# Calls of a two-block transformer kernel in another order on four engines, with triangular products and convolutions at each head's begin

## What is computed

```
# block 1
h = rms_norm(x, pre_w);  proj = h @ w_in               # 1024 x 6152
sb:  z = q k^T / 8;  log_a = log_sigmoid(z) + suffix sum of -softplus(z)   (causal)
     o_sb = (exp(log_a) @ v) * silu(gate)
gdn: q, k, v = silu(causal_depthwise_conv(qkv, conv_w));  q, k l2-normalized
     m = strict_lower(beta * k k^T * decay);  u, w = solve(I + m, [v beta, k beta exp(g)])
     for each chunk: v_new = u - w S;  o = q exp(g) S + intra v_new;  S = S exp(g_last) + k^T v_new
     o_g = rms_norm(o) * silu(gate)
y = (sigmoid(ma) * (o_sb @ w_sb) + sigmoid(mb) * (o_g @ w_gdn)) @ w_out;  x = x + rms_norm(y)

# block 2
h = rmsnorm(x);  proj = h @ w_in_2
diff: 4 heads, each of two softmaxes of 64:  o = rmsnorm((softmax(z1 + bias) - lam softmax(z2 + bias)) @ v)
fox:  8 heads of 64: softmax(q k^T / 8 + cum_q - cum_k) @ v     (cum: running sum of log sigmoid)
x = x + rmsnorm(concat(diff, fox) @ w_out_2)
x = x + rmsnorm(square(relu(rmsnorm(x) @ w_up)) @ w_down)
```

## Time and profile before

| | us |
|---|---|
| median of 3 runs | 1246.92 |
| lowest and highest | 1245.46, 1247.05 |
| the profiled execution | 1248.23 |
| its span | 1246.9 |
| TensorE busy in the span | 1188.6 (95%) |
| ScalarE, VectorE, GpSimd busy | 557.8, 518.8, 471.6 |

### The profile page before, as it was taken

One profiled execution on the slowest core, in us unless ns is written; L12 is line 12 of the kernel. 1 busy time (PEld: TensorE's weight loads), 2 busy tenths in 40 slices (PEclk: granted clock), 3 DMA queues, 4 the chain that ended last, 5 costly groups with the idle time before them and its releaser, 6 DMA issues.

```text
span 1246.9 us, 15061 instructions
## 1 busy us (share of the span) xinstructions
PE 1188.6 (95%) x5783; PEld 931.0 (75%) x5783; DVE 518.8 (42%) x1092; ACT 557.8 (45%) x1012; POOL 471.6 (38%) x291
## 2 busy tenths in 40 slices
PE   6999999999989999989999999989899999999997
PEld 6777767767657788878677777657888888888886
DVE  4057376575564314153233333332621111644444
ACT  5356466375477653243344444343432222433332
POOL 3344344234343344552222221222444444644441
PEclk9999999999999999989999999978899999999999
DMA  8221120211121233622111111111233333423211
GB/s 240 77 68 52 35 80 23 68 52 34 51 68 35 68 102 102 219 68 56 51 52 51 52 51 51 52 51 51 68 102 93 93 101 101 127 93 102 95 58 68
DMA packets 139801, 95.35 MB, mean 76 GB/s; under 512 B 8801, under 2 KB 124874, under 8 KB 139730
## 3 DMA queue, kind: packets, MB, share of 16 engines
q1 hardware_dynamic: 136112, 89.18, 24.5%
q10 hardware_dynamic: 3618, 5.22, 1.3%
HBM read 91.49 MB, written 2.88 MB: 76 GB/s over the span
## 4 chain that ended last, share of the span: by engine, by line
PE 84%; DVE 8%; ACT 4%; POOL 1%; issue 1%; DMA 0%; ACTq 0%; DVEq 0%
PE bank L411 24%; PE bank L1166 12%; PE bank L1148 12%; PE bank L440 5%; PE bank L808 4%; PE bank L817 3%; PE bank L833 2%; DVE g L1865 2%; PE bank L946 2%; PE bank L631 2%; PE bank L1179 1%; PE bank L958 1%; PE bank L622 1%; DVE g L1862 1%; PE bank L447 1%
## 5 line engine op out<-in xcount | busy, mean ns | idle before, releaser
L2388 POOL TENSOR_TENSOR ring<-raw_ring,ring 128x1024 fp32r<-128x1024 f32 x159 | 386.3, 2433 | 607.0 <-ACT ring L1192 607.0
L411 PE MATMUL bank<-hT,ring 128*128 128x512 f32 x1536 | 406.4, 410 | 4.1 <-POOL ring L2388 3.4
L411 PEld LDWEIGHTS bank<-hT,ring 128*128 128x128 f32 x1536 | 282.7, 192 | 75.0 <-issue 16.4
L1192 ACT CAST ring<-raw_ring 128x1024 fp32r<-128x1024 f32 x160 | 166.7, 1044 | 116.2 <-PE bank L1166 93.8
L1166 PE MATMUL bank<-ring,ring_u 128*128 128x512 f32 x672 | 154.0, 391 | 0.0
L1148 PE MATMUL bank<-hT,ring 128*128 128x512 f32 x672 | 152.5, 389 | 0.0
L1166 PEld LDWEIGHTS bank<-ring,ring_u 128*128 128x128 f32 x672 | 126.2, 188 | 27.6
L1148 PEld LDWEIGHTS bank<-hT,ring 128*128 128x128 f32 x672 | 126.1, 188 | 26.1
L2365 DVE TENSOR_TENSOR ring_u<-u,ring_u 128x1024 fp32r<-128x1024 f32 x32 | 82.4, 2582 | 76.0 <-ACT ring_u L1744 76.0
L2370 DVE TENSOR_TENSOR u<-u 128x512 f32<-128x512 f32 x32 | 22.9, 715 | 139.2 <-ACT u L1751 139.2
L440 PE MATMUL bank<-hT,ring 128*128 128x256 f32 x576 | 70.4, 284 | 2.3 <-DVE hT L1790 2.3
(11 more groups left out here) (297 smaller groups left out, 1615.2 us busy)
## 6 DMA issues: line engine op xcount, KB each, us to landing
raw_ring<-in_w_in SPq DMA_DIRECT2D x144, 256.0 KB, 3.3
raw_ring<-in_w_up SPq DMA_DIRECT2D x64, 256.0 KB, 3.3
raw_ring<-in_w_down SPq DMA_DIRECT2D x64, 256.0 KB, 2.8
raw_ring<-in_w_out SPq DMA_DIRECT2D x32, 256.0 KB, 2.8
x<-in_x SPq DMA_DIRECT2D x4, 512.0 KB, 5.7
raw_ring<-in_w_branch_sb SPq DMA_DIRECT2D x8, 256.0 KB, 2.9
raw_ring<-in_w_branch_gdn SPq DMA_DIRECT2D x8, 256.0 KB, 3.3
x<-in_x ACTq DMA_DIRECT2D x4, 512.0 KB, 6.0
```

The costliest lines, as they stand in the source:

```text
L411: p = pe.matmul(bank, m.slab_k8(n % 4)[:, a, k, :], m.hT[:, b, k, :], start=term == 0, stop=term == 23)
L1192: act.copy(m.ring[:, q, 0, :], m.raw_ring[:, q, :]).then_inc(s.slab_hi[q], 1)
L2388: pool.tensor_tensor(m.ring[:, q, 1, :], m.raw_ring[:, q, :], m.ring[:, q, 0, :].bitcast(F32), ALU.subtract).then_inc(s.slab_lo[q], 1)
```

## The change

No arithmetic is changed and no instruction is added or removed: TensorE runs the same 2400 matmuls of cover and the same small calls. The calls of TensorE, ScalarE, VectorE and GpSimd inside the heads of both blocks stand in another order, and the numbers in `tiles.to(n)` are others. In block 1 `stick_v_rows` moves to the begin of the head, `stick_av` of one head stands between the `stick_z` of the two, `delta_q_sum` comes 56 matmuls into the cover and not 48, and `stick_log` in the last head follows 33 cover matmuls after `stick_z`. On ScalarE `tile_a(g + 6)` moves ahead of `delta_out_high`, and the gate's silu to other places. In block 2 the differential head's half n = 1 starts first, and `fox_z(0)` comes after 37 cover matmuls. In the last head the 72 cover matmuls are spread to its end. At the start ScalarE casts slab 1, slab 0 and squares a third block of x before it copies the columns of the norm weights (`colp`), and VectorE makes slab 1's low part before it scales the second block of x. At the end the cast `split_u(31)` stands before the last weight's. The cover is cut into 218 stretches, 188 before. The line numbers of TensorE's calls after `Tall` in the changed kernel differ from before by up to 8, those of ScalarE by 21.

The diff, cut to what is spoken of:

```diff
@@ -642,61 +641,67 @@
 
     for i in range(3):
         tiles = Tall(SLABS_A + 8 * (i + 1), 8, tile_a_free(8 * (i + 1)))
-        tiles.to(14)
+        tiles.to(10)
+        stick_v_rows(i)
+        tiles.to(27)
         delta_decay(i)
-        tiles.to(27)
+        tiles.to(31)
         delta_decay_rows(i)
-        tiles.to(48)
+        tiles.to(56)
         delta_q_sum(i)
-        stick_v_rows(i)
-        tiles.to(60)
+        tiles.to(58)
+        stick_z(i, 1, 3)
         stick_z(i, 0, 3)
-        stick_z(i, 1, 3)
+        tiles.to(68)
         delta_k_sum(i)
+        tiles.to(75)
+        stick_log(i, 0, 3)
         delta_v_rows(i)
-        tiles.to(76)
-        stick_log(i, 0, 3)
-        stick_log(i, 1, 3)
         tiles.to(78)
         delta_gram(i)
-        tiles.to(88)
+        tiles.to(80)
+        stick_log(i, 1, 3)
+        tiles.to(86)
+        stick_av(i, 1, 3)
         stick_z(i, 0, 2)
+        stick_av(i, 0, 3)
         stick_z(i, 1, 2)
-        stick_av(i, 0, 3)
-        stick_av(i, 1, 3)
-        tiles.to(102)
+        tiles.to(100)
         stick_log(i, 0, 2)
+        tiles.to(105)
         stick_log(i, 1, 2)
-        tiles.to(105)
+        tiles.to(107)
         stick_z(i, 0, 1)
         stick_z(i, 1, 1)
         stick_av(i, 0, 2)
         stick_av(i, 1, 2)
-        tiles.to(126)
+        tiles.to(121)
         delta_level_first(i, 4)
         stick_log(i, 0, 1)
         stick_log(i, 1, 1)
         delta_level_second(i, 4)
+        tiles.to(122)
+        stick_av(i, 0, 1)
+        stick_z(i, 1, 0)
+        stick_av(i, 1, 1)
         stick_z(i, 0, 0)
-        stick_z(i, 1, 0)
-        stick_av(i, 0, 1)
-        stick_av(i, 1, 1)
-        tiles.to(128)
+        tiles.to(134)
         delta_level_first(i, 5)
-        tiles.to(140)
         stick_log(i, 0, 0)
         stick_log(i, 1, 0)
         delta_level_second(i, 5)
         stick_av(i, 0, 0)
         stick_av(i, 1, 0)
         delta_level_first(i, 6)
-        tiles.to(143)
+        tiles.to(137)
         delta_level_second(i, 6)
-        tiles.to(146)
+        tiles.to(140)
         delta_solve(i)
-        tiles.to(150)
+        tiles.to(144)
         delta_chunk(i, 0)
+        tiles.to(147)
         delta_from_state(i, 1)
+        tiles.to(149)
         delta_chunk(i, 1)
         tiles.to(152)
...
@@ -718,76 +723,78 @@
 
     i = 3
     tiles = Tall(SLABS_MERGE, 16, merge_free)
-    tiles.to(8)
+    tiles.to(1)
+    stick_v_rows(i)
     delta_decay(i)
-    tiles.to(18)
     delta_decay_rows(i)
-    tiles.to(20)
-    stick_v_rows(i)
-    tiles.to(56)
+    tiles.to(54)
     delta_q_sum(i)
-    tiles.to(64)
+    tiles.to(63)
     delta_k_sum(i)
+    tiles.to(71)
     delta_v_rows(i)
-    tiles.to(91)
+    tiles.to(83)
     delta_gram(i)
-    tiles.to(103)
+    tiles.to(84)
     stick_z(i, 0, 3)
...
@@ -967,78 +975,77 @@
 
     for i in range(3):
         tiles = Tall(SLABS_B + 6 * (i + 1), 6, tile_b_free(6 * (i + 1)))
-        tiles.to(13)
+        tiles.to(5)
         diff_v_rows(i, pairs)
-        tiles.to(18)
+        tiles.to(22)
+        diff_z(i, 1, 0, 0, pairs)
         fox_v_rows(i)
-        tiles.to(22)
+        tiles.to(25)
+        diff_z(i, 1, 0, 1, pairs)
         diff_z(i, 0, 0, 0, pairs)
         diff_z(i, 0, 0, 1, pairs)
-        diff_z(i, 1, 0, 0, pairs)
-        diff_z(i, 1, 0, 1, pairs)
         fox_decay(i, 0)
+        tiles.to(37)
         fox_decay(i, 1)
-        tiles.to(23)
         fox_z(i, 0, 0)
-        tiles.to(25)
+        tiles.to(38)
+        diff_rows_T(i, 1, 0, pairs)
         fox_z(i, 1, 0)
-        tiles.to(40)
+        tiles.to(48)
+        fox_rows_T(i, 1, 0)
+        tiles.to(51)
+        fox_av(i, 1, 0)
         fox_rows_T(i, 0, 0)
-        tiles.to(43)
-        fox_rows_T(i, 1, 0)
-        tiles.to(48)
+        diff_av(i, 1, 0, pairs)
+        tiles.to(54)
...
         diff_av(i, 1, 1, pairs)
-        tiles.to(118)
         fox_z(i, 0, 3)
+        tiles.to(119)
         fox_z(i, 1, 3)
+        tiles.to(128)
+        fox_rows_T(i, 0, 3)
         tiles.to(134)
-        fox_rows_T(i, 0, 3)
+        fox_rows_T(i, 1, 3)
+        tiles.to(137)
+        diff_mix(i, 4)
         tiles.to(138)
-        fox_rows_T(i, 1, 3)
+        fox_av(i, 1, 3)
         tiles.to(140)
-        diff_mix(i, 4)
+        fox_av(i, 0, 3)
         tiles.rest()
-        fox_av(i, 0, 3)
-        fox_av(i, 1, 3)
         fox_mix(i)
 
     class HeadsOut:
@@ -1068,65 +1075,79 @@
 
     i = 3
     tiles = HeadsOut()
-    tiles.to(15)
+    tiles.to(1)
     diff_v_rows(i, last_pairs)
     fox_v_rows(i)
-    tiles.to(22)
+    tiles.to(6)
     diff_z(i, 0, 0, 0, last_pairs)
+    tiles.to(7)
+    fox_decay(i, 0)
+    tiles.to(8)
+    diff_z(i, 0, 0, 1, last_pairs)
+    fox_decay(i, 1)
     diff_z(i, 1, 0, 0, last_pairs)
-    fox_decay(i, 0)
-    fox_decay(i, 1)
+    tiles.to(10)
...
+    tiles.to(54)
+    diff_z(i, 0, 1, 1, last_pairs)
     fox_rows_T(i, 1, 2)
-    diff_z(i, 0, 1, 1, last_pairs)
     fox_av(i, 0, 2)
+    diff_rows_T(i, 1, 1, last_pairs)
     fox_av(i, 1, 2)
     fox_z(i, 0, 3)
+    diff_rows_T(i, 0, 1, last_pairs)
     fox_z(i, 1, 3)
+    tiles.to(55)
+    diff_av(i, 0, 1, last_pairs)
+    tiles.to(58)
+    diff_av(i, 1, 1, last_pairs)
+    tiles.to(59)
     fox_rows_T(i, 0, 3)
+    tiles.to(60)
     fox_rows_T(i, 1, 3)
-    diff_rows_T(i, 0, 1, last_pairs)
-    diff_rows_T(i, 1, 1, last_pairs)
-    diff_av(i, 0, 1, last_pairs)
-    diff_av(i, 1, 1, last_pairs)
+    tiles.to(63)
     fox_av(i, 0, 3)
     fox_av(i, 1, 3)
     diff_mix(i, 5)
+    tiles.to(64)
     fox_mix(i)
+    tiles.to(72)
 
     pe.wait_ge(s.d_mix, 4)
     pe.wait_ge(s.f_mix, 4)
...
@@ -1228,16 +1249,16 @@
 
     first_squares(0)
     first_squares(1)
+    split(SLABS_A + 1)
+    split(SLABS_A)
+    first_squares(2)
     act.wait_ge(s.cols_T, 1)
     act.copy(m.colp[:, 0:73], banks[2][:, 0:73]).then_inc(s.cols, 1)
-    split(SLABS_A)
-    split(SLABS_A + 1)
     act.wait_ge(s.cols, 1)
     act.wait_ge(s.memsets, 4)
     norm_high(0, 0, m.prew_col)
-    first_squares(2)
+    split(SLABS_A + 2)
     first_squares(3)
-    split(SLABS_A + 2)
     split(SLABS_A + 3)
     norm_high(0, 1, m.prew_col)
...
         delta_norms(i)
         tile_a(g + 2)
         stick_exp(i, 0, 3)
+        delta_mT(i)
         stick_exp(i, 1, 3)
-        log_of_sigmoid(gate, m.rawg, s.g_sig, 4 * i)
-        delta_mT(i)
         stick_soft(i, 0, 2)
         stick_soft(i, 1, 2)
         tile_a(g + 3)
@@ -1412,7 +1432,7 @@
         stick_exp(i, 1, 2)
         stick_soft(i, 0, 1)
         stick_soft(i, 1, 1)
-        exponential(gate, s.g_dve, 2 * i + 1, s.g_sig)
+        log_of_sigmoid(gate, m.rawg, s.g_sig, 4 * i)
         delta_level(i, 4)
         stick_exp(i, 0, 1)
         stick_exp(i, 1, 1)
@@ -1421,6 +1441,7 @@
         stick_soft(i, 1, 0)
         tile_a(g + 4)
         delta_level(i, 5)
+        exponential(gate, s.g_dve, 2 * i + 1, s.g_sig)
         stick_exp(i, 0, 0)
         stick_exp(i, 1, 0)
         delta_level(i, 6)
@@ -1428,8 +1449,8 @@
         delta_w(i)
         tile_a(g + 5)
         delta_out(i)
+        tile_a(g + 6)
         delta_out_high(i)
-        tile_a(g + 6)
         tile_a(g + 7)
 
...
@@ -1641,45 +1662,45 @@
         g = 6 * (i + 1)
         diff_v(i, 2)
         fox_v(i)
-        diff_exp(i, 0, 0, 0)
-        diff_exp(i, 0, 0, 1)
+        tile_b(g)
+        fox_decay(i, 0)
         diff_exp(i, 1, 0, 0)
         diff_exp(i, 1, 0, 1)
-        fox_decay(i, 0)
         fox_decay(i, 1)
+        diff_p(i, 1, 0, 4)
+        diff_exp(i, 0, 0, 0)
         fox_exp(i, 0, 0)
-        tile_b(g)
         fox_exp(i, 1, 0)
+        diff_exp(i, 0, 0, 1)
+        fox_p(i, 1, 0)
         fox_p(i, 0, 0)
-        fox_p(i, 1, 0)
         tile_b(g + 1)
         diff_p(i, 0, 0, 2)
...
@@ -1762,8 +1783,8 @@
     split_u(29)
     split(SLABS_DOWN + 30)
     split_u(30)
+    split_u(31)
     split(SLABS_DOWN + 31)
-    split_u(31)
     act.wait_ge(s.post_in, 48)
     for j in range(NT):
         row_squares(2, j, 0, 4 + j, m.scr4)
@@ -1794,13 +1815,13 @@
     dve.memset(m.eps_c, EPS).then_inc(s.memsets, 1)
     dve.memset(m.one_c, 1.0).then_inc(s.memsets, 1)
     dve.memset(m.half_c, -0.5).then_inc(s.memsets, 1)
-    dve.memset(m.cin[:, :, 0:4], 0.0).then_inc(s.memsets, 1)
     norm_scale(0, 0, m.x1, m.scr, 0)
-    norm_scale(0, 1, m.x1, m.scr, 0)
     dve.wait_ge(s.slab_hi[1], 1)
     dve.tensor_tensor(m.ring[:, 1, 1, :], m.raw_ring[:, 1, :], m.ring[:, 1, 0, :].bitcast(F32), ALU.subtract).then_inc(s.slab_lo[1], 1)
+    norm_scale(0, 1, m.x1, m.scr, 0)
+    dve.memset(m.cin[:, :, 0:4], 0.0).then_inc(s.memsets, 1)
+    norm_scale(0, 2, m.x1, m.scr, 0)
     norm_low(0, 0, m.prew_col)
-    norm_scale(0, 2, m.x1, m.scr, 0)
     norm_scale(0, 3, m.x1, m.scr, 0)
```

More of the change, by code:

```diff
@@ L708, in tensor_program @@
         delta_chunk(i, 3)
-        tiles.to(165)
+        tiles.to(166)
         delta_o_sum(i)
@@ L992, in tensor_program @@
-        fox_av(i, 1, 0)
-        tiles.to(54)
+        tiles.to(62)
```

(37 more changed lines are left out.)

351 lines of the change are left out of this document (175 added, 176 removed).

## The result

The changed kernel takes 1216.05 us (median of 4 runs, 1215.39 to 1216.33) against 1246.99 before (4 runs): a ratio of 0.9753, 95% interval 0.9736 to 0.9770, so 31 us or 2.5% faster. The forecast was 1225. The profiled execution has a span of 1215.0, before 1246.9.

The account below looks back on a forecast made before the run. TensorE was taken as the bound, with time in its gaps, clock and call pairing. -17.6 - 10.2 - 14.7 + 10 + 3 + 2.7 + 3.2 + 1.5 = -22.1 took 1246.9 to 1225 us (chance 0.62); range 1213 to 1238.

Parts of the forecast that it names:

- Block 1, waits and clock (-17.6): Block 1's heads: all large TensorE waits but the 2.9 in delta_gram go, 13.6 us, plus 4 us of clock.
- the stretches: TensorE's cover in the whole kernel: 30 more pieces at 0.09 us each add 2.7 us.
- The wait ahead of `delta_q_sum`: Block 1's heads: 5.0 us of waiting for ScalarE's squares goes, through earlier convolutions and eight more cover matmuls, 1.8 us.
- Lone calls in block 1 (+10): stick_z and stick_av of two heads no longer run in pairs, so second calls cost full length: 5.5 to 10, taken as 10.
- Lone calls in block 2 (+3): diff_z and fox_z in block 2 no longer run in pairs: 2.1 to 4.8 us added, taken as 3.
- The waits and the clock of these heads (-10.2): Block 2's first three heads: waits at fox_z and fox_mix go, 5.6 us, plus 4.6 us of clock.
- The last head (-13 and -1.7): Block 2's last head: spread cover brings it to 46.6 us, -13; the 24 matmuls behind it at full clock, -1.7.
- Startup (+3.2): Program start: slab 1's cast and low part come first, first projection moves from 13.76 to 17.6; adds 3.2 us, bounds 2 to 4.2.
- Slips (+1.5): Whole kernel: some of fifty calls in new places won't fit, bringing new waits; 1.5 us added, from nothing to 6.
- ScalarE's queue: Block 1's first heads: moved activations delay delta_level_second and TensorE's queue, 27 us added, 1252; chance 0.07.
- The last head did shrink: Judges the rival that block 2's last head doesn't shrink, set by its softmax chain with low clock: 1238, chance 0.15.
- Free lone calls, the first rival: Both blocks: split calls overlap other work, slips don't come and startup hides, giving 1212; chance 0.12.

Follow-up runs that it names:

- the ScalarE edit: Kernel before, with the next head's second-slab cast and tile copy ahead of delta_out_high's cast in block 1's first three heads; 1242.78 us, ratio 0.9972.
- the head of 84.95 us: Second head of block 1, in old order, in the kernel before with only block 2's first three heads reordered; that kernel took 1237.43 us, ratio 0.9924.

## Why the prediction was right, and where its terms were off

**The bound and the signs** held. TensorE's waits go, its clock rises in the heads, and the added costs are where they were put. The measured gain is 31 and the forecast was 22, so the direction and the mechanism were right and the size was near one end of the range. The terms were further off than their sum: block 1 gave 6.7 us more than was forecast and the three heads of block 2 some 2 more, the norms gave 2.4 that stood in no term, and the last head gave 3.8 less. That these partly cancel is luck.

**Block 1, waits and clock (-17.6).** This is the term that was too small. The forecast for these heads was -17.6, the 10 of lone calls and about 1.8 of the stretches, -5.8 together; they gave -12.5. The windows of the four heads split this. Idle time fell from 17.1 us to 5.0, by 12.2, new waits included, where 13.6 was forecast. Three heads had a clock of 0.98, 1.7 us each and 5.1 in all, and after the change none has; 4 was taken. (The window that the prediction took for the last head, 327 to 461 us, reaches past it; in the head itself, 319.87 to 424.78, the clock is 0.98 and not 0.99. In block 2 its window is that of the second head, not of the third, which has the same length within 0.1.) (That it is the new order which keeps the clock up is seen over all traces: of the nine second, third and last heads of block 1 in the old order, in three traces, eight have such a fall of the clock, and of the 24 in the new order, in eight traces, none. Which of the waits does it is not shown.) The lone calls cost 9.6. What is left is busy time, which fell by 4.8 where 1.8 of stretches had been added. This 6.6 is the term that the prediction did not have: it priced a wait at the idle time in its brackets. The views count 22 waits in these heads before, 8 after. For six of these fourteen, two in each of the first three heads, the price beyond the idle time was measured: 0.6 for two together with the two stretches allowed for, so 0.3 each. If the other eight cost the same, which was not tried, it is 14 x 0.3 = 4.2, and 2.4 stay open.

**The wait ahead of `delta_q_sum`.** The prediction let the earlier cast on ScalarE bring the convolutions forward, and the longer cover do the rest. The trace of the ScalarE edit bears the first part out: the step ahead of `delta_q_sum` ended 1.3 us sooner. But the same edit takes away the wait at the head's begin and so brings TensorE there sooner as well, which the prediction did not say; alone it took 0.3 of the 5.0.

**Lone calls in block 1 (+10)**: 9.6, taken back by pairing them. Right, and right to take the bound at which nothing overlaps. The trace shows no added price for alternating calls on half the rows with calls on half the columns: a lone `stick_av` takes 0.79 us to the next start and a lone `stick_z` 1.05, and a pair of each took the same, 0.79 and 1.06, with half as many changes in all. The two also stand to each other as their columns do (384 to 512), which leaves nothing fixed for a change unless it is hidden in both. By the rule of the Trainium skill that I set against it (TensorEngine Tiling (Array Packing), Key Properties: changing the mode drains) it should have been more; no such term is seen here.

**Lone calls in block 2 (+3)** cost close to nothing, 0.1 to 0.2 a head in the sums of `diff_z` and `fox_z`. What went wrong was to look for the partner only among calls of the same kind. The new order puts a `diff_z` of one half of the rows beside a `fox_z` of the other, and they run together:

```profile
686.05 0.48 PE L920 MATMUL bank<-b,b 64*128 64x256 f32 x1
686.06 0.59 PE L954 MATMUL bank<-b,b 64*128 64x384 f32 x1
686.37 0.38 PE L920 MATMUL bank<-b,b 64*128 64x256 f32 x1
686.49 0.48 PE L954 MATMUL bank<-b,b 64*128 64x384 f32 x1
```

The waits and the clock of these heads (-10.2) were right: the net was -9.4, forecast -7.2 before stretches, and the difference is about this term.

**The last head (-13 and -1.7).** It gave 9.1 from `fox_mix` to `fox_mix` and 1.9 behind it. Its chain of softmaxes did not become the bound; no wait stands in it behind the 1.7 at its begin. This is 11.0 of the 14.7 forecast, and the head is over the 48 us that were named as the sign of being right. What is missing is clock: the prediction took nearly full clock, and this head had 0.87. The order alone gave 12.2 and 1.9 in its own experiment, 14.1, close to the forecast, with the same calls and a shorter stretch at half clock; the longer one costs 3.1.

**Startup (+3.2)** was 3.0, with the first projection at 17.49 where 17.6 was worked out; the first transposes began at 12.94, by the column copy, and not at 13.5 by VectorE.

**Not in the sum**: the two norms behind the blocks' ends ran 1.2 us shorter each, since less of them fell on half clock (in the first 20 us of each, 0.93 and 0.91 where it was 0.87 and 0.85). No edit stands there, so this too is no work of the new order that is shown. **Slips (+1.5)**: new waits of 1.2 and 0.9 in block 1.

**The rivals.** ScalarE's queue, which would have made it slower, shows in no wait: the thin slack at the triangular products was enough. The last head did shrink. Free lone calls, the first rival, held for block 2 and not for block 1; its 1212 is nearer to the result than the forecast, but mostly for other reasons.

**What stays open**: where the clock falls. It fell in the last head in every kernel, by 0 to 3 us more or less, in other places of the same calls, and in stretches that an edit had not touched. In the head of 84.95 us it did not fall behind two waits behind which it fell in others. The experiments tell what it costs, not what sets the place. The first three heads of block 2 are the clear case: all twelve in the old order, in four traces, have a fall of the clock, and none of the 24 in the new order. So the clock's part of the gain there and in block 1, some 5 us each, is the new order's as a whole, though not one wait's, and that of the norms and of the last head's 3 us can't be put down to an edit.
